# Transposed copies of x, memory and context in place of TensorE transposes, first loads in another order, and mLSTM weights by direction

## The reference

```
def hybrid_layer(x, mem, pos, g_mix, w_in, ..., g_mem, w_mkv, g_mlp, w_up, w_down):
    h = rms_norm(x, g_mix)
    z = h @ w_in                                  # queries, keys, values, gates
    o_a = dilated_mixer(...)                      # windowed attention
    o_b = moba_attn(...)                          # block attention
    o_m = memory_attn(q_m * scale, rms_norm(mem, g_mem), w_mkv)
    y = gates[0] * (o_a @ w_pa) + gates[1] * (o_b @ w_pb) + gates[2] * (o_m @ w_pm)
    x = x + y @ w_o
    return x + jnp.square(jax.nn.relu(rms_norm(x, g_mlp) @ w_up)) @ w_down
```

```
    mod_l = jax.nn.silu(c) @ w_mod[l] + b_mod[l]
    mod_c = jax.nn.silu(c_ctx)[None, :] @ w_mod[l] + b_mod[l]
    h_l = modulate(rmsnorm(x, norm1[l]), sh1, sc1)       # h * (1 + scale) + shift
    h_c = modulate(rmsnorm(ctx, norm1[l]), sh1c, sc1c)
    out_c, out_l = mixer(h_c, h_l, ...)                  # mLSTM: decays forward and backward
    ...
    # experts: softmax over 16, each takes its top 32 tokens, silu(x @ gate) * (x @ up) @ down
```

## Time and profile before

| | |
|---|---|
| median of 3 runs | 1577.0 us (1576.68 to 1578.81) |
| the profiled execution | 1576.6 us |
| its span in the trace | 1574.8 us |
| TensorE busy | 1428.4 us, 91% |
| ScalarE, VectorE, GpSimd busy | 35%, 37%, 43% |
| DMA | 395.40 MB, mean 251 GB/s |

### The profile page before, as it was taken

How to read it: one execution, slowest core, us unless ns; L and a number is a source line. 1 busy time by engine, 2 the same in 40 slices (tenths; PEclk the granted TensorE clock), 3 DMA queues, 4 the chain that set the end, 5 groups by cost and what they waited for, 6 DMA issues and landing times.

```text
span 1574.8 us, 17946 instructions
## 1 busy us (share of the span) xinstructions
PE 1428.4 (91%) x7601; PEld 1015.6 (64%) x7601; DVE 578.9 (37%) x885; ACT 551.9 (35%) x709; POOL 673.6 (43%) x187
## 2 busy tenths in 40 slices
PE   8999999999999999999999999999996676666666
PEld 7877788877887778887799888978841121121111
DVE  4532423336262242334743886768510010010001
ACT  6356443433535545434343344574310000000001
POOL 5846588755784658786555775010000000000000
PEclk9999999999999999999999999999997788787788
DMA  8534457588553445659825444014999999999997
GB/s 296 188 112 157 149 173 240 182 304 315 174 182 126 146 147 183 226 181 337 320 87 183 147 145 154 14 68 142 419 407 427 427 429 427 427 428 428 428 427 292
DMA packets 115517, 395.40 MB, mean 251 GB/s; under 512 B 5719, under 2 KB 9620, under 8 KB 101996
## 3 DMA queue, kind: packets, MB, share of 16 engines
q1 hardware_dynamic: 113372, 388.70, 66.3%
q0 software_dynamic: 1520, 4.49, 0.8%
q10 hardware_dynamic: 544, 1.05, 0.2%
HBM read 393.16 MB, written 1.05 MB: 250 GB/s over the span
## 4 chain that ended last, share of the span: by engine, by line
PE 76%; DMA 20%; DVE 2%; ACT 1%; issue 1%; SPq 0%; DVEq 0%; ACTq 0%
PE psum L2284 18%; PE psum L2286 17%; PE psum L2285 17%; DMA ring<-in_w_e_down 7%; PE psum L1249 7%; DMA ring<-in_w_e_gate 6%; DMA ring<-in_w_e_up 6%; PE psum L1164 2%; PE psum L2437 1%; PE psum L2464 1%; PE psum L1025 1%; PE psum L2328 1%; PE psum L2513 1%; PE psum L824 1%; PE psum L823 1%; PE psum L825 1%
## 5 line engine op out<-in xcount | busy, mean ns | idle before, releaser
L655 POOL TENSOR_TENSOR ring_lo<-ring,ring_hi 128x2048 fp32r<-128x2048 f32 x118 | 537.9, 4565 | 230.5 <-ACT ring_hi L635 230.3
L635 ACT ACTIVATE ring_hi<-ring 128x2048 fp32r<-128x2048 f32 (+1 forms) x127 | 239.9, 1889 | 317.4 <-DMA ring<-in_w_down 108.5
L2286 PE MATMUL psum<-ring_hi,hT_hi 128*128 128x512 f32 (+2 forms) x848 | 327.7, 386 | 0.0
L2285 PE MATMUL psum<-ring_lo,hT_hi 128*128 128x512 f32 (+2 forms) x848 | 327.0, 386 | 0.0
L2284 PE MATMUL psum<-ring_hi,hT_lo 128*128 128x512 f32 (+2 forms) x816 | 323.0, 396 | 0.6 <-DVE ring_lo L2638 0.2
L1249 PE MATMUL psum<-arena 128*32 128x512 f32 x796 | 142.9, 706 | 64.2 <-DMA arena<-in_w_e_down 23.4
L1249 PE MATMUL psum<-ring,arena 128*32 128x512 f32 x720 | 132.8, 727 | 60.2 <-DMA ring<-in_w_e_gate 23.0
L2286 PEld LDWEIGHTS psum<-ring_hi,hT_hi 128*128 128x128 f32 x848 | 159.2, 188 | 32.4
L2285 PEld LDWEIGHTS psum<-ring_lo,hT_hi 128*128 128x128 f32 x848 | 159.5, 188 | 28.6
L2284 PEld LDWEIGHTS psum<-ring_hi,hT_lo 128*128 128x128 f32 x816 | 153.3, 188 | 37.6 <-issue 6.8
L1249 PEld LDWEIGHTS psum<-arena 128*32 128x32 f32 x796 | 32.2, 127 | 164.9 <-issue 73.6
(11 more groups left out here) (467 smaller groups left out, 1930.3 us busy)
## 6 DMA issues: line engine op xcount, KB each, us to landing
ring<-in_w_in SPq DMA_DIRECT2D x59, 1024.0 KB, 5.1
ring<-in_w_up SPq DMA_DIRECT2D x32, 1024.0 KB, 5.5
ring<-in_w_down SPq DMA_DIRECT2D x32, 1024.0 KB, 5.3
ring<-in_w_e_down SPq DMA_DIRECT2D x16, 2048.0 KB, 20.4
arena<-in_w_e_up SPq DMA_DIRECT2D x14, 2048.0 KB, 20.6
arena<-in_w_e_down SPq DMA_DIRECT2D x12, 2048.0 KB, 23.5
ring<-in_w_e_gate SPq DMA_DIRECT2D x12, 2048.0 KB, 22.7
arena<-in_w_e_gate SPq DMA_DIRECT2D x12, 2048.0 KB, 22.9
```

The lines of the kernel that those rows point to most:

```text
L635: act.activation(slot_hi(u)[:, 0:c, :], slot(u)[:, 0:c, :], ACT.Copy).then_inc(hi_sb, 1)
L655: eng.tensor_tensor(slot_lo(u)[:, 0:c, :], slot(u)[:, 0:c, :], slot_hi(u)[:, 0:c, :].bitcast(F32), ALU.subtract).then_inc(done, 1)
L2285: pe.matmul(dst, hi(k0 + k), w_lo, start=False, stop=False)
L2286: last = pe.matmul(dst, hi(k0 + k), w_hi, start=False, stop=stop and k == nk - 1)
```

## The change

Four more arrays come from the host: x, memory and context transposed (x_t, mem_t, ctx_t) and the gain norm_mix as 16 columns (gain_cols).

- Start: ScalarE's queue loads half of xT ahead of x's place; SP loads gain_cols and the constants, unit 0 in four pieces, unit 1 in two halves, the rest of xT, then units 2 and 3 and the small rows. ScalarE and VectorE read xT instead of accumulators. TensorE has no transposes of x and gain, and a `second_unit` that goes by halves. x itself is loaded by ScalarE's queue once unit 2 has landed. VectorE makes the low part of unit 2.
- Memory: its 16 transposes are dropped in both layers. Memory and memT are loaded by GpSimd between its low parts of units 3, 4 and 5 in layer 0; in layer 1 SP loads memT behind unit 3. ScalarE copies memT into flat[2] and flat[3].
- Context: ctxT, 1 MB more, is loaded behind the context. TensorE drops the 8 + 8 transposes and adds two matmuls that spread the context's norm over partitions; VectorE multiplies ctxT by it, and ScalarE modulates ctxT into the accumulators, four steps per half.
- mLSTM: `weights` waits by direction; ScalarE makes `em` ahead of ring_hi.

```diff
-LO_VECTOR = [(l, u) for l in range(DEPTH) for u in SPLIT if (l == 0 and u < 2) or (u >= 50 and u % 4 == 2)]
+LO_VECTOR = [(l, u) for l in range(DEPTH) for u in SPLIT if (l == 0 and u < 3) or (u >= 50 and u % 4 == 2)]
...
             def weights(h):
-                dve.wait_ge(dec_a, 10 * h + 10)
                 for d, a, b in ((0, 0, 768), (0, 896, 1024), (1, 0, 640), (1, 768, 1024)):
+                    dve.wait_ge(dec_a, 10 * h + 5 * d + 5)
...
-                if h + 1 < MH:
-                    high_parts(U_OUT - U_IN + h + 1, U_OUT - U_IN + h + 1)
                 if h == 0:
                     act.wait_ge(at_full, 2)
...
+                if h + 1 < MH:
+                    high_parts(U_OUT - U_IN + h + 1, U_OUT - U_IN + h + 1)
...
             pool.dma_start(ctx_x, w["ctx_2"].rearrange("b (t p) d -> p (b t) d", p=P)).then_inc(rows_in, 16)
+            pool.dma_start(ctxT, w["ctx_t"].rearrange("(c p) t -> p c t", p=P)).then_inc(rows_in, 16)
...
+            sp.dma_start(cols[:, 0:16], w["gain_cols"]).then_inc(const_in, 16)
             sp.dma_start(consts[:, 0:P], w["consts"][:, 0:P]).then_inc(const_in, 16)
-            gain_rows(0, "norm_mix", const_in)
...
+                        sp.dma_start(xT[:, 4:8, :], x_src[:, 4:8, :]).then_inc(rest_in, 16)
...
+                    if l and u == R1 - 1:
+                        sp.dma_start(memT, w["mem_t"].rearrange("(c p) t -> p c t", p=P)).then_inc(late_in, 16)
...
+            def second_unit():
+                for half in range(2):
+                    pe.wait_ge(lo_v, UC + half + 1)
...
             pe.wait_ge(const_in, 32)
-            pe.transpose(psum[:, 7, 0:16], rows1[0:16, :], ident[0:16, 0:16]).then_inc(cols_full, 1)
-            pe.wait_ge(x_in, 16)
-            half_to_features(x, 0)
-            keep_busy(6, 4)
+            keep_busy(6, 5)
             first_unit()
-            pe.wait_ge(rest_in, 16)
-            half_to_features(x, 1)
+            second_unit()
...
-                pe.wait_ge(mem_in, 32)
-                to_features(mem_tok)
...
-                        if l + 1 == DEPTH and u == 61:
-                            half_to_features(ctx_x, 0)
-                        if l + 1 == DEPTH and u == 62:
-                            half_to_features(ctx_x, 1)
...
+                            pe.wait_ge(norm_v, 2)
+                            for t in range(TT):
+                                last = pe.matmul(psum[:, 4, t * P:(t + 1) * P], stat[:, t, 3:4].to_broadcast([P, P]), ident,
+                                                 start=True, stop=True)
...
+                    for half in range(2):
+                        v = ctxT[:, 4 * half:4 * half + 4, :]
+                        dve.tensor_tensor(v, v, psum[:, 4, 0:T].unsqueeze(1).to_broadcast([P, 4, T]), ALU.mult).then_inc(mod_sb, 1)
...
+            act.wait_ge(slot_in[2], 16)
+            act.dma_start(x[:, :, :], w["x"].rearrange("b (t p) d -> p (b t) d", p=P)).then_inc(x_in, 16)
...
+                    high_parts(6, 6)
...
+                    act.wait_ge(rows_in, 16)
...
+                for half in range(2):
+                    act.activation(flat[2 + half].rearrange("p (k t) -> p k t", k=4), memT[:, 4 * half:4 * half + 4, :], ACT.Copy)\
+                       .then_inc(mem_f, 1)
...
-            pool.wait_ge(rest_in, 16)
-            pool.wait_ge(slot_in[2], 16)
-            pool.dma_start(mem_tok, w["mem"].rearrange("b (t p) d -> p (b t) d", p=P)).then_inc(mem_in, 16)
-            pool.dma_start(consts[:, P:], w["consts"][:, P:]).then_inc(mem_in, 16)
...
                     split_lo(pool, l, u)
+                    if l == 0 and u == 3:
+                        pool.wait_ge(x_in, 32)
+                        pool.dma_start(mem_tok, w["mem"].rearrange("b (t p) d -> p (b t) d", p=P)).then_inc(mem_in, 16)
+                    if l == 0 and u == 4:
+                        pool.dma_start(memT, w["mem_t"].rearrange("(c p) t -> p c t", p=P)).then_inc(rows_in, 16)
+                    if l == 0 and u == 5:
+                        pool.wait_ge(mem_in, 16)
+                        pool.dma_start(consts[:, P:], w["consts"][:, P:]).then_inc(mem_in, 16)
```

More of the change, by code:

```diff
@@ L324, in build @@
         mem_in = sem("mem_in")
+        mem_f = sem("mem_f")
         sq_a = sem("sq_a")
@@ L376, in build @@
         out_done = sem("out_done")
-        ctx_x = carve(23808, TT, D)
+        ctx_x = carve(20480, TT, D)
+        ctxT = carve(23808, KC, T)
         final_row = carve(22784, D)
-        ctx_junk = [carve(20480 + D * t, D) for t in range(TT)]
         modrow = carve(0, 3, UN)
@@ L2345, in first_unit @@
                 last.then_inc(slots_free, 1)
+            def second_unit():
+                for half in range(2):
+                    pe.wait_ge(lo_v, UC + half + 1)
+                    for t in range(TT):
+                        last = split_product(DB[1][:, t, :], tokens(hT_hi, t), tokens(hT_lo, t), 2 * half, 1, nk=2, first=2 * half,
+                                             start=half == 0, stop=False)
+                last.then_inc(slots_free, 1)
             def late_rows():
@@ L2571, in _, with low_half @@
         def _(dve):
-            def low_half(half, gain, ready):
+            def low_half(half, gain, ready, features=None):
                 for k in range(4):
@@ L2646, in _ @@
                 low_piece(k)
-            split_lo(dve, 0, 1)
+            for half in range(2):
+                cs = slice(2 * half, 2 * half + 2)
+                dve.wait_ge(hi_sb, UC + half + 1)
+                dve.tensor_tensor(slot_lo(1)[:, cs, :], slot(1)[:, cs, :], slot_hi(1)[:, cs, :].bitcast(F32), ALU.subtract).then_inc(lo_v, 1)
             for l in range(DEPTH):
-                low_half(1, g_feat[:, 0, l, :], l * 18 + 4)
+                low_half(1, g_feat[:, 0, l, :], l * 18 + 4, None if l else xT)
@@ L2663, in _ @@
+                dve.tensor_scalar(means[:, cs], means[:, cs], 1.0 / D, EPS, ALU.mult, ALU.add).then_inc(r_v, 1)
+                dve.wait_ge(sq_a, l * 12 + 5)
+                dve.reciprocal(r_x, roots[:, cs]).then_inc(r_v, 1)
+                dve.wait_ge(r_v, l * 9 + 3)
                 dve.tensor_scalar(half_r, r_x, 0.5, None, ALU.mult).then_inc(r_v, 1)
@@ L2680, in _ @@
                 z_tile(1)
+                if l == 0:
+                    cm = slice(TT, 2 * TT)
+                    dve.wait_ge(sq_a, 7)
+                    dve.tensor_scalar(means[:, cm], means[:, cm], 1.0 / D, EPS, ALU.mult, ALU.add).then_inc(r_v, 1)
+                    dve.wait_ge(sq_a, 8)
+                    dve.reciprocal(r_mem, roots[:, cm]).then_inc(r_v, 1)
+                    dve.wait_ge(r_v, 6)
                 for half in range(2):
-                    dve.wait_ge(turn_full, l * 8 + 3 + half)
+                    dve.wait_ge(mem_f, 2 * l + half + 1)
                     for k in range(4):
```

229 lines of the change are left out of this document (131 added, 98 removed).

## The result

The changed kernel takes 1589.05 us (median of 5 runs, 1586.91 to 1591.56), the kernel before 1577.32 us in the same session (5 runs, 1576.68 to 1578.99). The ratio is 1.0071, 95% interval 1.0060 to 1.0083. The prediction was 1571.5 us, faster; the time lies outside its range of 1567.8 to 1574.5 and on the other side of no change.

What follows compares the result with a forecast made beforehand. TensorE bounds the kernel until 1050 us, loads the expert stage. Start −2.8, memory in layer 1 −1.74, context +0.6, mLSTM −1.14 sum to −5.08, from 1576.6 to 1571.5 us; 8-in-10 range 1567.8 to 1574.5.

Steps and rivals of the forecast that it cites:

- What bounds the kernel: Whole kernel: TensorE is saturated from 40 to 1050 us; the expert stage is bound by loads that wait for earlier events.
- Start and first memory: Layer 0 up to unit 8: earlier start and dropped transposes, less losses by late loads, −2.8 us (−0.3 to −4.3).
- just hidden: GpSimd's low parts at the start: low part plus load issue takes 5.43 us against TensorE's 5.45 a unit.
- late x: Start: x, issued once unit 2 has landed, shares the engines with unit 3's load; a loss of 0 to 1.0 us.
- ideal of 52.2: Start without losses by late loads: unit 8 begins at 52.2 us instead of 56.5, 4.3 us gained.
- Memory in layer 1: Memory's 16 transposes in layer 1 go, the extra load is hidden: −1.7 us.
- Context: Context in layer 1: TensorE's terms net −1.3, a stall of 1.9 for loads; sum +0.6 us (−1.3 to +1.1).
- stall for w_mod: Modulation behind unit 51 of layer 1: ctxT's extra 1 MB load delays w_mod, 1.9 us (0 to 2.4).
- mLSTM: Wait for ScalarE's L2047 at 1061.34 us falls as exponentials go first: −1.1 us (−0.9 to −1.2).
- Expert stage: Last stage, from 1145 us: same length, so that any earlier shift passes through to the end.
- The one that ended slower: Rival, 5%: transposed memory's load lands from 17.1 us after issue, ScalarE waits before unit 7's high part; above 1580.2 us.
- Theory A: From the experiments, not the prediction: a VectorE instruction that reads and writes SBUF alone waits for GpSimd.

Runs made afterwards that it cites:

- v2: Changed kernel without VectorE's SBUF-to-SBUF instructions in the first ten units, ScalarE's order changed, ctxT loaded by SP behind unit 61 of layer 1: 1579.35 us, ratio 1.0008.
- v3_ctx_gpsimd: As v3, but with ctxT loaded on GpSimd's queue behind the context, as the change has it: 1574.13 us, ratio to the kernel before 0.9979.
- v3: As v2, with one more wait on GpSimd, ahead of unit 10's low part in layer 0, for VectorE's eight rope steps: 1571.73 us, ratio 0.9958.
- e2: Changed kernel with one more wait on GpSimd, behind unit 4's low part, until VectorE has halved silu_c: 1586.49 us, ratio 1.0059.
- e4: Kernel before with five more VectorE instructions as probes, at a time when GpSimd runs low parts: 1576.65 us, one run.
- after_pauses: Changed kernel with only three more waits on GpSimd, for the halving of silu_c, the memory's means and the rope steps: 1580.11 us, ratio 1.0014.
- e1: Changed kernel with VectorE's two halvings (half_r, silu_c) moved behind z_tile(2) and z_tile(3) of layer 0: 1588.48 us, ratio 1.0072.

## Why the prediction was wrong, by its steps

**What bounds the kernel: incomplete.** "A microsecond of TensorE work removed is a microsecond gained, provided that the producers keep the new pace" holds, but I counted as producers only those that make high and low parts, and priced each by its own duration. VectorE's duration depends on what GpSimd does in the same moment (0.30 or 10.41 us for the same halving). The first part of the prediction names no such link.

**Start and first memory: wrong, −2.8 forecast, +13.6 measured at unit 8.** Two terms failed, both ahead of unit 4, where the prediction counts no loss. The bigger one is VectorE's. The step prices GpSimd's load issues between the low parts by GpSimd's time alone, "just hidden". That came out: the low parts start 5.49 and 5.04 us apart. But it puts VectorE's small steps ahead of unit 4 at nothing, and the only spare time that it counts on VectorE is the "about 4 us" at unit 8's accumulator. With GpSimd's pause at 30.46 to 33.16 gone, the halvings were held until 44.25, and unit 4 started 12.0 us behind its low part. The cover that the change took away was not that of the loads alone, but also GpSimd's idle moment. The smaller term is x's. Its bullet prices the late x by unit 3 only, at 0 to 1.0 us; there it cost nothing, and no unit 6 waited either. It missed that ScalarE's squares of x stand ahead of unit 4's high part, which cost 2.0 us in the changed kernel's trace.

The rest of the step was near: TensorE began at 7.72 (7.4 forecast; the first six matmuls were 0.43 apart, the slow pace of the prediction) and reached unit 2 at 20.45 (19.5). v2, with VectorE free and two high parts moved out from behind the late loads, reached unit 8 at 52.92, close to the ideal of 52.2 (the kernel before: 56.72, where the prediction has 56.5).

**Memory in layer 1: right.** The lag falls from 13.6 us at unit 8 of layer 0 to 12.0 at unit 5 of layer 1, −1.6 against −1.7.

**Context: mechanism right, size too small.** The terms on TensorE came out (17.7 at unit 52 to 15.2 in the mLSTM, less 1.1 for that, is −1.3, as forecast). The stall for w_mod was put at 1.9, up to 2.4; it measured 3.7 and 1.8 more of slow pace in the changed kernel, 3.4 in v3_ctx_gpsimd. I had counted one more MB of loading; the slow pace behind a wait, and a bigger delay than the bytes account for, were missing. Net of all, the context's part costs time as it is; with the load elsewhere its terms on TensorE come out the same in v3's trace (−1.4).

**mLSTM: right at its place**, 1.14 forecast, 1.16 measured alone, of which 0.67 reached the end of that one trace.

**Expert stage: right.** The shift of 15.2 us passes through to 15.0 at the end.

**The rivals.** The one that ended slower put the loss on transposed memory behind ScalarE, from 17.1 us on; ScalarE did wait 10.63 us there, but for VectorE's means, not for the load. Theory A is shown by e2, e4, v3 and after_pauses, for the 12.0 us at unit 4 and for the rope steps. Not settled are why four runs of e1 lost 9 us, and what exactly decides whether VectorE or GpSimd's next low part comes first.

## What to carry to other kernels

Where VectorE and GpSimd both work in SBUF, a tiny VectorE instruction can cost as much as GpSimd's whole queue ahead of it. Look through the page before for VectorE groups whose mean is far above what their elements explain (here 128x384 products of 2.77 us that take 0.56 us alone), and for small ones that end with a GpSimd instruction (L2659, 128x4, took 0.64 us and ended at 30.49, a low part at 30.46). Ask of every change that fills a gap of GpSimd which VectorE instruction used that gap. Such steps go to ScalarE, into an instruction that reads PSUM, or behind a wait that gives VectorE the moment: one wait on GpSimd bought 7.6 us here (v2 to v3). And follow a load that is moved late to all that stands behind it in its engine's order, not only to the next unit.
